# Row sums read their conditions from PSUM, GpSimd takes part of the weight splits, and the row sums are dealt to other chunks

## The reference, cut to what matters

```python
def ada_modulation(cond, w, b):          # cond: c_ctx for the context, c for the latents
    m = jax.nn.silu(cond) @ w + b        # w: 2048 x 6144 for each layer
    shift, scale, gate = jnp.split(m[:, None, :], 3, axis=-1)
...
hp = rms_norm(xp, norm_pre[l]) * (1.0 + scale_p) + shift_p
...   # a mixer: projections of h, the mixing, an output projection
xp = xp + gate_p * rms_norm(op, norm_post[l])
```

## Time and profile before

| | us |
|---|---|
| median of 3 runs | 3196.59 (3186.47 to 3199.36) |
| the profiled execution | 3185.92 |
| its span, first to last instruction | 3184.1 |
| TensorE / VectorE / ScalarE / GpSimd busy | 2946.0 / 2116.8 / 1043.0 / 216.7 |
| mean granted clock of TensorE | 0.966 |

### The profile page before, as it was taken

How to read it: one execution, slowest core, us unless ns; L and a number is a source line. 1 busy time by engine, 2 the same in 40 slices (tenths; PEclk the granted TensorE clock), 3 DMA queues, 4 the chain that set the end, 5 groups by cost and what they waited for, 6 DMA issues and landing times.

```text
span 3184.1 us, 46787 instructions
## 1 busy us (share of the span) xinstructions
PE 2946.0 (93%) x18927; PEld 2585.6 (81%) x18927; DVE 2116.8 (66%) x4191; ACT 1043.0 (33%) x1399; POOL 216.7 (7%) x346
## 2 busy tenths in 40 slices
PE   5799999999999999899998988997998999999998
PEld 2588889967778999789877767986777999997777
DVE  4599977944786667649886875565587774235444
ACT  1434333233324232233324423223324222323332
POOL 2034440000000210000000000000000000000000
PEclk7899999999999999899999999998899999999999
DMA  9899996611464996867654444553365665421132
GB/s 375 311 332 351 354 326 225 228 54 54 152 228 167 251 273 227 316 264 267 244 199 164 163 146 146 185 196 120 145 227 178 216 215 174 131 93 54 54 132 93
DMA packets 242535, 639.17 MB, mean 201 GB/s; under 512 B 22400, under 2 KB 55840, under 8 KB 217232
## 3 DMA queue, kind: packets, MB, share of 16 engines
q1 hardware_dynamic: 215232, 524.58, 47.5%
q0 software_dynamic: 27088, 111.61, 9.9%
HBM read 564.16 MB, written 71.91 MB: 200 GB/s over the span
## 4 chain that ended last, share of the span: by engine, by line
PE 68%; DVE 16%; DMA 7%; ACT 4%; DVEq 2%; issue 2%; ACTq 1%; POOL 0%; SPq 0%; POOLq 0%
PE bank L357 33%; PE bank L361 16%; DVE w_lo L540 4%; DMA raw<-in_ada_w 3%; DVE bank L449 3%; PE bank L927 3%; PE bank L921 3%; DVE raw L449 2%; ACT w_hi L533 2%; PE bank L942 2%; DVE arena L2211 1%; PE bank L968 1%; PE bank L2586 1%; PE bank L946 1%; DMA s_in_dram<-arena 1%
## 5 line engine op out<-in xcount | busy, mean ns | idle before, releaser
L540 DVE TENSOR_TENSOR w_lo<-raw,w_hi 128x2048 fp32r<-128x2048 f32 (+2 forms) x352 | 617.6, 1770 | 509.7 <-ACTq L534 505.4
L533 ACT ACTIVATE w_hi<-raw 128x2048 fp32r<-128x2048 f32 (+2 forms) x352 | 520.1, 1495 | 1187.5 <-PE bank L357 607.7
L357 PE MATMUL bank<-hT_hi,w_hi 128*128 128x384 f32 (+1 forms) x2608 | 885.7, 340 | 22.7 <-DVEq L541 9.6
L357 PE MATMUL bank<-hT_hi,w_lo 128*128 128x384 f32 (+1 forms) x2608 | 876.1, 336 | 0.0
L357 PE MATMUL bank<-hT_lo,w_hi 128*128 128x384 f32 (+1 forms) x2608 | 875.8, 336 | 0.0
L357 PEld LDWEIGHTS bank<-hT_hi,w_hi 128*128 128x128 f32 (+1 forms) x2608 | 491.0, 188 | 39.2 <-issue 23.2
L357 PEld LDWEIGHTS bank<-hT_lo,w_hi 128*128 128x128 f32 (+1 forms) x2608 | 491.3, 188 | 1.2
L357 PEld LDWEIGHTS bank<-hT_hi,w_lo 128*128 128x128 f32 (+1 forms) x2608 | 490.8, 188 | 1.0
L361 PE MATMUL bank<-w_hi,hT_hi 128*128 128x512 f32 x1056 | 422.0, 400 | 29.7 <-DVE arena L1238 14.2
L361 PE MATMUL bank<-w_hi,hT_lo 128*128 128x512 f32 x1056 | 417.8, 396 | 0.0
L361 PE MATMUL bank<-w_lo,hT_hi 128*128 128x512 f32 x1056 | 417.1, 395 | 0.0
(11 more groups left out here) (342 smaller groups left out, 2986.0 us busy)
## 6 DMA issues: line engine op xcount, KB each, us to landing
raw<-in_ada_rows SPq DMA_DIRECT2D x128, 1024.0 KB, 5.0
raw<-in_ada_w SPq DMA_DIRECT2D x64, 1024.0 KB, 8.9
raw<-in_mla_w_in SPq DMA_DIRECT2D x64, 768.0 KB, 7.5
raw<-in_gla_w_in SPq DMA_DIRECT2D x48, 1024.0 KB, 5.2
raw<-in_mla_w_in SPq DMA_DIRECT2D x40, 1024.0 KB, 5.3
raw<-in_mla_w_out SPq DMA_DIRECT2D x32, 1024.0 KB, 5.2
raw<-in_s_w_in SPq DMA_DIRECT2D x32, 1024.0 KB, 8.1
s_out_dram<-arena POOLq DMA_DIRECT2D x32, 512.0 KB, 5.8
```

Source lines behind the costliest of these rows:

```text
L357: mm = nc.tensor.matmul(banks[m][0:width, 0:TOK], wp[:, k, at:at + width], hp[:, kt, :], start=(first and n == 0), stop=(last and n == 2))
L533: nc.scalar.activation(dst, src_, ACT.Copy)
L540: nc.vector.tensor_tensor(dst, src_, pick(w_hi, *part)[0], ALU.subtract)
```

## The change

1. **Conditions.** The first step of every set copies condition 0 into bank 4 and, for the sets in `SILU_PLACED`, condition 1 into bank 5. All row sums read them from there. The product for condition 0 goes to a place in SBUF (`products_of`). So each operation has one input in SBUF and one in PSUM.
2. **GpSimd splits.** The low part is made by GpSimd for gate0 chunks 3 to 9, out0, out1 and out2 chunks 1 to 15, and glu1 chunks 2 to 15, 66 in all. In the output stages chunk 1 stands ahead of `fetch_x` in GpSimd's order, the others behind it. The rest stay with VectorE.
3. **Other chunks.** Nine sets become eight. Gated linear attention has four groups of row sums instead of seven, with none in `va` group 1, `r0`, `r2`, `r3`; out0, out1 and out2 have four groups each instead of three, over chunks 1 to 13; the set of gate0 begins with `krope0`; that of glu1 ends at chunk 14. `out2` now loads its conditions in `fetch_x`.

```diff
-    gla = [(f"{name}2", n, s) for name, groups in GLA_ORDER for n in range(groups) for s in range(4)]
-    return [(range(16, 20), chunks("gate0", 0, 16), (13824, 14336, 22144)),
-            (range(20, 23), chunks("out0", 1, 13), (12928, 13632, 13448)),
-            (range(23, 27), chunks("u1", 1, 16) + chunks("gate1", 0, 11), (4608, 5120, 5632)),
-            (range(27, 31), chunks("glu1", 1, 16), (19200, 19712, 20224)),
-            (range(31, 34), chunks("out1", 1, 13), (12928, 13632, 13448)),
-            (range(34, 38), gla[:24], (12928, None, 13448)),
-            (range(38, 41), gla[28:47], (12928, None, 13448)),
-            (range(41, 44), chunks("out2", 1, 13), (12928, None, 13448)),
-            (range(44, 48), chunks("q3", 1, 31), (9216, 9728, 10240))]
-SILU_PLACED = {0: 0, 1: 1, 2: 2, 3: 3, 4: 4, 8: 5}
+    gla = {("qa2", 0): (2, 2, 2, 2), ("ka2", 0): (2, 2, 2, 2), ("va2", 0): (2, 2, 0, 0), ("r1_2", 0): (3, 3, 3, 3),
+           ("qb2", 0): (3, 3, 3, 3), ("kb2", 0): (3, 3, 3, 3), ("vb2", 0): (3, 3, 2, 0)}
+    def evenly(groups, keys):
+        n = 16 * len(groups)
+        return groups, [keys[i * len(keys) // n] for i in range(n)]
+    out_place = (12928, 13632, 13448, 14144)
+    return [evenly(range(16, 20), [("krope0", 0, 0)] + chunks("gate0", 0, 15)) + ((13824, 14336, 22144, 13824),),
+            evenly(range(20, 24), chunks("out0", 1, 14)) + (out_place,),
+            evenly(range(24, 28), chunks("u1", 1, 16) + chunks("gate1", 0, 11)) + ((4608, 5120, 5632, 4608),),
+            evenly(range(28, 32), chunks("glu1", 1, 15)) + ((19200, 19712, 20224, 19200),),
+            evenly(range(32, 36), chunks("out1", 1, 14)) + (out_place,),
+            (range(36, 40), [key + (s,) for key, counts in gla.items() for s in range(4) for _ in range(counts[s])],
+             (12928, 13632, 13448, 12928)),
+            evenly(range(40, 44), chunks("out2", 1, 14)) + (out_place,),
+            evenly(range(44, 48), chunks("q3", 1, 31)) + ((9216, 9728, 10240, 9216),)]
+SILU_PLACED = {0: 0, 1: 1, 2: 2, 3: 3, 4: 4, 6: 5, 7: 6}
...
                 if f in SILU_PLACED:
                     nc.vector.wait_ge(silu_in, 16 + 64 * (SILU_PLACED[f] + 1))
+                nc.vector.tensor_copy(banks[4][:, :], silu_placed(f, 0))
+                if f in SILU_PLACED:
+                    nc.vector.tensor_copy(banks[5][:, :], silu_placed(f, 1))
+                nc.vector.drain()
...
-                nc.vector.scalar_tensor_tensor(out=got if c else banks[5][:, :], in0=got, scalar=1.0, in1=silu_of(f, c), op0=ALU.mult,
+                nc.vector.scalar_tensor_tensor(out=got if c else products_of(f), in0=got, scalar=1.0, in1=banks[4 + c][:, :], op0=ALU.mult,
...
+            elif eng == "pool":
+                nc.gpsimd.wait_ge(hi_ready, n + 1)
+                nc.gpsimd.wait_ge(lo_ready, n)
+                for part in parts:
+                    dst, src_ = pick(w_lo, *part)
+                    nc.gpsimd.tensor_tensor(dst, src_, pick(w_hi, *part)[0], ALU.subtract).then_inc(lo_ready, 1)
             else:
                 nc.vector.wait_ge(hi_ready, n + 1)
+                if by_pool(n - 1):
+                    nc.vector.wait_ge(lo_ready, n)
...
+        def by_pool(n):
+            name, g, s = dense[n] if n >= 0 else ("", 0, 0)
+            first, end = {"gate0": (3, 10), "out0": (1, 16), "glu1": (2, 16), "out1": (1, 16), "out2": (1, 16)}.get(name, (99, 99))
+            return first <= 4 * g + s < end
+        def pool_splits(name, first, end):
+            for n in range(first, end):
+                split_chunk("pool", name, n // 4, n % 4)
...
-            if n < len(dense):
+            if n < len(dense) and not (eng == "dve" and by_pool(n)):
                 split_chunk(eng, *dense[n])
...
-            if l < 2:
-                pool_silu(pool, (1, 4)[l])
+            if l != layers[-1]:
+                pool_silu(pool, (1, 4, 5)[l])
...
+                if l != layers[-1]:
+                    pool_splits(f"out{l}", 1, 2)
                 fetch_x(pool, l)
+                if l != layers[-1]:
+                    pool_splits(f"out{l}", 2, 16)
...
                 pool_silu(pool, 0)
+                pool_splits("gate0", 3, 7)
             pool.wait_ge(kv_normed, nth(l) + 1)
             nc.gpsimd.dma_start(outs[2][0, j], ckv_sb[:, 0, :]).then_inc(stored, 16)
+            if l == 0:
+                pool_splits("gate0", 7, 10)
```

## The result

| | us |
|---|---|
| before, median | 3195.6 (3186.5 to 3199.4, 4 runs) |
| after, median | 3148.2 (3143.7 to 3153.2, 4 runs) |
| ratio | 0.9862, 95% interval 0.9847 to 0.9877 |
| predicted | 3142, range 3110 to 3182 |
| profiled execution after | 3153.2, span 3151.4 |

The change makes the kernel 47 us faster by the medians; 54 were forecast. The two profiled executions differ by only 32.7 us in their spans: the one of before (3185.9 us) was faster than any of the four in the table, and the one of after is the slowest of its four.

The account below looks back on a forecast made before the run. TensorE, busy for 93% of the span, was taken as the bound, losing time to idleness and low clock as VectorE's work queued behind row sums. Terms summed to -54.2 us, from 3196.6 to 3142, range 3110 to 3182.

Parts of the forecast that it names:

- four units, wait and clock: Head recurrences in gated linear attention: fewer row sums ahead cut TensorE's waits for `decayed` by 29.4 us, higher clock 4.
- `va`: Value projection in gated linear attention: losing 17 of 21 row-sum steps saves 14 us, with 3 left for a ScalarE hold-up.
- three output stages: Output projections of layers 0 to 2: 33.8 us of excess go, new waits at the starts cost 29.8; net -4.0.
- `krope0` and `gate0`: Layer 0's gate stage: -6.2 us at its end, +3.4 where sums delay the rotary key's eviction; together -2.8.
- the chain of three engines: Ahead of each unit, work passing between ScalarE and VectorE while TensorE runs leaves a wait of about 1.9 us.
- only the 4.0 us of the sums go: Rival for the units: the chain through ScalarE keeps its place, units give 16 us, not 33; 3159 us, chance 0.18.
- the 4 to 8 that the prediction named as a sign: Output stages of layers 0 to 2: each should have one wait of 4 to 8 us behind its second chunk.
- the starts cost nothing: Rival for the output stages: no new wait at their starts, 29.8 us more gained; 3113 us, chance 0.10.
- GpSimd's splits: 66 low parts moved to GpSimd: about 4.5 us each, within 5.9 us free in a steady chunk; cost 0.
- the rival of 6.7 us a split: Rival: GpSimd is slower than the chunk, the 66 splits cost 53 us and time stays 3197; chance 0.07.
- The conditions in PSUM: Row sums with one PSUM input: same pace, copies of 11 us lie in VectorE's slack; 0, bounds ±2.
- GpSimd and VectorE shut each other out: Rival: splits and row sums can't overlap in output stages, GLU and gate0; +134 us, 3277, chance 0.10.

Follow-up runs that it names:

- ahead_of_units: Changed kernel with the same 64 steps of row sums in gated linear attention, 48 of them dealt ahead of the units again; 3189.8 us, ratio 0.9995.
- best2: best1 with the 4 row-sum steps behind `va` 0.0 and 0.1 dealt to `r1` instead; 3101.0 us, ratio 0.9716.
- start2: conds_first with the row-sum sets of the three output stages over chunks 2 to 14 instead of 1 to 13; 3115.6 us, ratio 0.9763.
- conds_first: Changed kernel with chunk 1's low part in the three output stages back on VectorE, so GpSimd sends conditions and x first; 3120.0 us, ratio 0.9775.
- on_vector: Changed kernel with all 66 low parts back on VectorE, dealing of sums and conditions in PSUM kept; 3172.9 us, ratio 0.9948.
- sbuf_on_vector: Changed kernel with conditions read from SBUF and all 66 low parts on VectorE, no arithmetic on GpSimd; 3170.4 us, ratio 0.9933.
- conds_sbuf: Changed kernel with row sums outside gated linear attention reading both conditions from SBUF, GpSimd's splits kept; 3267.1 us, ratio 1.0237.
- no_krope: Changed kernel with layer 0's gate set of row sums begun behind `gate0`'s first chunk instead of behind `krope0`; 3141.2 us, ratio 0.9840.
- best1_b: best1 run once more, beside best2_b on the same chip; 3108.9 us, ratio 0.9738.
- best2_b: best2 run once more, beside best1_b on the same chip; 3103.4 us, ratio 0.9722.
- best1: Changed kernel with conditions sent before GpSimd's first split, output sets over chunks 2 to 14, gate set behind `gate0`'s first chunk; 3117.1 us, ratio 0.9766.

## Why the prediction was right, and where its sizes were off

The measured ratio moved as forecast, and 3148 is 6 us from 3142. By the stages of the traces, though, the change gave 13 us less than the sum:

| term | forecast | measured |
|---|---|---|
| four units, wait and clock | -33.4 | -34.9 |
| `va` | -14 | -10.0 |
| three output stages | -4.0 | +3.9 |
| `krope0` and `gate0` | -2.8 | -0.4 |
| sum | -54.2 | -41.4 |

**The units** were right in mechanism and size. The waits are 1.9, 1.6, 1.9 and 1.6 us, where the chain of three engines was taken to leave 1.9 each (its times, T + 12.5 less T + 10.8, give 1.7), and the clock rose with them. `ahead_of_units` brings the waits back to 38.0 us, and the rival "only the 4.0 us of the sums go" (3159, and 3168 for that run) falls.

**`va`** was right in mechanism, with the rest too small. I left 3 us for the place where ScalarE's exponential holds up a high part; the stage keeps 7.3 us over its 65.3 us of matmuls, of which 4.6 are that wait, and the clock of 0.95 behind it is most of what is left. The two steps ahead of the absolute value made 2.7 of the 4.6, as `best2` shows.

**The output stages.** This is the term that was mis-sized most: -4.0 forecast, +3.9 measured. Both halves of it exist. VectorE's excess in the steady part is gone: chunks follow each other at 8.16 us, and `start2` takes 130.0 us for `out0` (138.9 before). But what is left at the starts was put at 29.8 us and is 37.7 (13.8, 11.7 and 12.2 over the 129.8 of a stage without sums), and the waits of 9.1, 8.0 and 8.0 us lie at or above the upper end of the 4 to 8 that the prediction named as a sign. What was missing: the last transfer of the conditions takes 7.4 us rather than 5.0; TensorE waits 1.5 us in `out0` for GpSimd's split of chunk 1 as well; and the first chunks of `out1` and `out2` take 12.1 and 11.7 us in the kernel before, 11.6 and 12.1 after and 11.6 each in `start2`, against 9.98 in layer 3. In that of `out1` TensorE is busy throughout, at a granted clock of 0.82 before and 0.85 after and in `start2`. So 3 to 4 of the 33.8 us of excess did not come from VectorE's sums. The lowered clock behind the wait had been counted with 1.8 us; in `out0` the two chunks behind it take 2.7 us more than without a wait. `conds_first` takes 28 of the 37.7 away. The rival "the starts cost nothing" (3113) falls for the change, and `start2` (3115.6) comes near it.

**`gate0`.** The end gave its -6.2 us: from chunk 0.2 to the end of the stage 125.1 us against 131.3. The start was put at +3.4 and is +5.8: 3.6 for the eviction, near the 3.4 worked out, and 2.2 for the first gate chunk, in whose first 4.6 us, behind the wait of 4.37 us, a matmul takes 0.52 us instead of 0.33, at a granted clock of 0.50, the lower of its two levels; this had not been counted.

**GpSimd's splits** cost nothing in steady chunks: they take 4.63 us of a gap of 5.9, and 1.25 us are left ahead of TensorE (0.5 behind the end of a group). So the rival of 6.7 us a split falls. **The conditions in PSUM** were put at 0 with bounds of ±2. By themselves this holds (`on_vector` and `sbuf_on_vector` are equal within their intervals), but the gain hangs on them: the rival "GpSimd and VectorE shut each other out", given 0.10, is what happens without them. Its time was 3277 and `conds_sbuf` took 3267; it put 134 us on the lock, and 116 were measured.

**The medians** moved by 47 us and the four stages by 41. The other stages of the two profiled executions differ by 9 us the other way, 5 of them behind the gate projection of layer 1. Most likely that is an execution's own: this stage up to `glu1`, whose code is the same in all kernels but the one before and the two with the conditions in SBUF, took 266.2 to 267.9 us in six of the fourteen profiles (that of before, `start2`, `no_krope` and `best1_b` among them) and 269.2 to 273.2 in eight (`best2` and `best2_b` among them). So the sum of the stages can't be held against the medians to better than some 10 us. That 3148 came so near 3142, when the stages gave 13 us less than forecast, is in part luck.

## What to carry to other kernels

Before an engine with slack takes over work, look at what its queue sends at that moment: a split of 4.5 us ahead of four small transfers cost 9 us at each of three starts, and giving it back to VectorE gave 28 us. Deal filler work, here the row sums, away from chains that hop between engines; there six operations of 3.9 us cost 7.8 us each time. And where GpSimd computes beside VectorE, let VectorE read one of its inputs from PSUM; here that was worth 116 us.

## What the runs showed of the hardware that was not expected

The lock between VectorE and GpSimd holds one instruction until the other has ended: 5.08 us for an operation of 0.69. With conditions in PSUM none of the 1024 row sums is held, and the longest takes 691 ns. But the changed kernel still meets the lock in VectorE instructions that read two inputs from SBUF. Here are two of one line in the GLU's stage (a product with the gate), in order of time, GpSimd's splits beside them:

```profile
1452.62 1.75 DVE L2800 TENSOR_TENSOR arena<-arena 128x1536 f32<-128x1536 f32 x1
1453.25 5.61 POOL L554 TENSOR_TENSOR w_lo<-raw,w_hi 128x2048 fp32r<-128x2048 f32 x1 [2.95 <-ACTq L547]
...
1519.81 4.61 POOL L554 TENSOR_TENSOR w_lo<-raw,w_hi 128x2048 fp32r<-128x2048 f32 x1 [2.54 <-ACTq L547]
1520.70 5.33 DVE L2800 TENSOR_TENSOR arena<-arena 128x1536 f32<-128x1536 f32 x1
```

Whoever began first took its usual time, and the other was held: once the split (5.61 us instead of 4.63), once VectorE (5.33 instead of 1.75). Without GpSimd's splits, in `on_vector`, this line takes 1.75 us. It costs TensorE no wait that shows: the GLU takes 138.7 us, and 139.9 in `on_vector`.

The granted clock differs between executions in stretches with the same code. The stretch behind the gate projection of layer 1 in `start2`, then in `best1`:

```profile
1255.00:1387.40 132.40, 110.35 (x2426) 97.02 (x2424) 71.06 (x313) 41.77 (x73) 1.06 (x2) 0.95 0.83 317
...
1252.00:1389.70 137.70, 116.28 (x2428) 101.97 (x2426) 71.90 (x313) 41.65 (x73) 1.07 (x2) 0.90 0.80 305
```

The same matmuls, 5.3 us more, at a clock of 0.90 instead of 0.95. TensorE has short idle times throughout this stretch. All of the difference is TensorE's busy time (116.28 us against 110.35), not its idle time. What decides between the two wasn't found. The two medians of `best1`, taken on two chips, are 8 us apart (3117.1 and 3108.9), and the gate projection of layer 1 up to `glu1` takes 272.7 and 267.8 us in their profiles; so edits worth 5 us are judged by their stages.
